# The gated one-hot columns of the expert gates spread over ScalarE, GpSimd and VectorE

## The chip, the cores and the metric

One NeuronCore of a Trainium2 chip runs the whole kernel in one launch. The metric is device microseconds of that core. The core's engines are TensorE (PE in the profile; its weight loads are PEld), VectorE (DVE), ScalarE (ACT), GpSimd (POOL) and SyncE (SP). Each works through its own queue in order and meets the others at semaphores.

## The reference, cut to what matters

A decoder trunk of two layers over 512 tokens of width 1024, in float32. Each layer has a token mixer (two kinds of attention) and then a PEER sub-layer: for every token, 8 heads each pick 16 of 128 x 128 = 16,384 experts, one expert being a row of `u` and a row of `v`.

```
expert_idx = i_top[..., 0] * 128 + i_top[..., 1]      # 8 heads x 16 picks = 128 picks a token
gates = softmax(best)
act = gelu(h . u[expert_idx]) * gates                 # one number a pick
out = sum over the picks of act * v[expert_idx]
```

Half of the tokens (256) are done by fetching the picked rows from DRAM. For the other half the kernel computes `gelu(u h)` for all 16,384 experts and multiplies it by a gate map: for a token, the gate map G[i, j] is the gate of expert (i, j), and zero where the expert was not picked. As each pick k has a first key i(k), a second key j(k) and a gate g(k), the map is a product of two matrices with the 128 picks as the contracted side: P[k, x] = (x == one key of pick k) * g(k), and Q[k, y] = (y == the other key of pick k). This change is about the making of P.

## The kernel before

**The stages of a layer.** After the token mixer, `channel_mix` runs on every engine. TensorE (1) turns 64 of the 128 tiles of `u` and multiplies them with the tokens (`act_tiles`), (2) makes the gate maps of the 256 dense tokens (`gate_maps`), (3) multiplies the gated activations with 64 tiles of `v` (`value_tiles`), (4) does the other 64 tiles of `u`, and (5) the other 64 of `v`. The change touches stage 2 alone.

**The gate stage.** 256 tokens are 32 batches (`NB`) of 8 (`BATCH`). For a batch, `p1` holds P (8 tokens x 128 columns, two buffers, `s = b % 2`) and `q1` holds Q in the same shape. `pqgT` holds, for each token, three columns with a value for each of the 128 picks on the partitions: the two keys and the gate; a fourth holds the negated gate. `iota` is a 128 x 128 tile with 0 to 127 along each row. Batch b runs like this:

- ScalarE, `p_batch` (lines 945 and 949): P of tokens 0 to 5 (`P_ACT = 6`), two operations a token: Abs(key - iota), a drain, then Relu(gate - gate * that), which is the gate where the keys agree and zero elsewhere.
- VectorE, `q_batch` (lines 1425, 1427, 1431): P of tokens 6 and 7 in two `tensor_tensor` operations over both tokens (equal, and times the gate), and Q of all 8 tokens in one `tensor_tensor` of 1024 columns.
- TensorE (line 588) waits for `p_done`, `q_done`, `gm_done` and `gs_done`, multiplies 8 pairs of matrices (16 instructions in the profile) into two PSUM banks and counts `g_done`.
- VectorE, `gate_batch` (line 1441): multiplies the 64 columns of the present half into the activations, straight out of PSUM. ScalarE, `keep_batch` (line 961), copies the other half to SBUF afterwards, and SyncE writes it to DRAM for stage 4.

P and Q of batch b wait until TensorE is done with batch b - 2, whose buffer they take. VectorE's order is P and Q of batch b, gate of batch b - 1, one row, and so on; ScalarE's is P of batch b, copy of batch b - 1.

**The fetched rows.** Between all this VectorE works off 512 rows a layer (1024 columns each): a row of `u` with a multiply-and-sum (line 1408), a row of `v` with a multiply-add (line 1414) and a drain. GpSimd fetches them by an indirect DMA each (line 1155) into a ring of 8: the fetch of row r waits until row r - 8 is used up. In the gate stage VectorE does one row a batch: row 164 + b in batch b. At row 192 (batch 28) it also has a `topk` of some thirty small operations to do.

**After the stage.** Rows 196 to 367 are done beside stages 3 and 4. From row 368 on (`kept_maps`, line 1458) VectorE multiplies the kept half of the gate maps into the second half of the activations, for which it waits until TensorE has made them.

Of the kernel before, what the change touches and what calls it, by code (L numbers as in the profile page):

```python
# [25 lines left out]
ALU = mybir.AluOpType  # L26
# [3 lines left out]
P = 128  # L30
# [25 lines left out]
ND = CH - GCH  # L56
# [3 lines left out]
STREAM = 4  # L60
STREAMED = 2 * TILES
BATCH = 8
P_ACT = 6
NB = NT // BATCH
BLOCKS = 4
G_START = 302
# [46 lines left out]
def build(nc, io, out):  # L113
    with ExitStack() as ctx:
        def sb(name, shape, dt=F32):
            return ctx.enter_context(nc.sbuf_tensor(name, shape, dt))

        def sem(name):
            return ctx.enter_context(nc.semaphore(name))
# [76 lines left out]
        p1 = mod[:, SHIFT1:GAIN1 + 1, :]  # L196
# [7 lines left out]
        pqgT = h_row[:, :].rearrange("p (a b) -> p a b", a=4)  # L204
        at = [A_TOPK]

        def small(*dims):
# [29 lines left out]
        iota = sb("iota", [P, P])  # L237
# [5 lines left out]
        S = {n: sem(n) for n in (  # L243
            "c_in const_in x_in c_sig_done c_act_done zeros_done layer_done small_in lam_summed lam_exped g_in "
            "norm_gain bias_in mod_mm mod_evac acc_done sq_done sq2_done norm_h tr_done hT_ev "
            "q_ev k_ev v_ev dqraw_ev dkraw_ev dv_mm dv_ev rope_mm dq_ready dk_ready "
            "z_done  ln_done L_done b_done w_exp w_masked pv_done ysb_ev "
            "s_done max_done p_exp dw_done wt_done wt_ev y_done y_sq yn_done yt_done yd_ev "
            "sig_done merged_done wout_in wo_done x_upd "
            "query0_done qst0_ev sc0_done sc0_ev query_done qst_ev sc_done sc_ev topk_done gate_exp dots_done gelu_done "  # L250
            "row_used st_used ut_done ut_ev a_used a_ev iota_mm iota_ev td_done exp_t_done pre_done pt_done pq_ev p_done q_done g_done gm_done gs_done kept_used "
            "x_out x_back out_sq out_ready out_done "
            "parked_act parked_dve parked_pool parked_pe parked_sp").split()}
        ada_in = [sem(f"ada_in{i}") for i in range(3)]
# [199 lines left out]
        def _(pe):  # L454
# [123 lines left out]
            def gate_maps(l):  # L578

                with pe.Fori(0, NB // 2) as g:  # L580
                    for s in range(2):
                        b = NB * l + 2 * g + s
                        pe.wait_ge(S["p_done"], b + 1)
                        pe.wait_ge(S["q_done"], b + 1)
                        pe.wait_ge(S["gm_done"], b + 1)
                        pe.wait_ge(S["gs_done"], b + 1)
                        for t in range(BATCH):
                            last = pe.matmul(ps[:, G_BANK[s] + t // 4, t % 4 * P:(t % 4 + 1) * P],  # L588
                                             p1[:, s, t * P:(t + 1) * P], q1[s][:, t * P:(t + 1) * P], start=True, stop=True)
                        last.then_inc(S["g_done"], 1)  # L590
# [174 lines left out]
            with pe.Fori(0, DEPTH) as l:  # L765
# [10 lines left out]
                with pe.Fori(0, MT // 2) as m2:  # L776
                    for s in range(2):
# [3 lines left out]
                        for b, (k0, n, rhs) in enumerate(((0, KD, hT), (KD, KD, hT), (16, 4, y_sb), (20, 4, y_d))):  # L781
                            for k in range(n):
                                last = pe.matmul(ps[:, 4 * s + b, :], w_m[:, s, k0 + k, :], rhs[:, k, :],  # L783
                                                 start=(k == 0), stop=(k == n - 1))
# [30 lines left out]
                act_tiles(l, 0, 8 * (HEADS - 2), HALF)  # L815
                turn_picks(l)
                gate_maps(l)
                value_tiles(l, 0)
                turn_u(l, 1, 0)
# [5 lines left out]
        def _(act):  # L825
            def park():
                act.sem_inc(S["parked_act"], 1)
# [110 lines left out]
            def p_batch(l, b):  # L938
# [3 lines left out]
                park()  # L942
                for t in range(P_ACT):
                    n = BATCH * b + t
                    act.activation(p1[:, s, t * P:(t + 1) * P], iota[:, :], ACT.Abs, bias=pqgT[:, 1, n:n + 1], scale=-1.0)  # L945
                act.drain()
                for t in range(P_ACT):
                    n = BATCH * b + t
# [173 lines left out]
        @block.gpsimd  # L1122
        def _(pool):
            def park():
                pool.sem_inc(S["parked_pool"], 1)

            with pool.Fori(0, DEPTH) as l:
                with pool.Fori(0, TURNS) as t:
                    i = l * TURNS + t
                    for u in range(2 * CH):  # L1130

                        pool.wait_ge(S["w_exp"], 8 * i + u + 1)
                        park()
                        pool.affine_select(out=w_att[:, u % 2, 0:P], in_=w_att[:, u % 2, 0:P], compare_op=ALU.is_gt,  # L1134
                                           fill=0.0, base=0, pattern=[[1, P]], channel_multiplier=-1
                                           ).then_inc(S["w_masked"], 1)
                def read_kept(r, half):
                    slot = r % KEPT
                    pool.wait_ge(S["kept_used"], 2 * NB * l + NB * half + r + 1)
                    park()  # L1140
                    if half == 0 and r < KEPT:
                        pool.wait_ge(kept_out[slot], 16 * (NB // KEPT) * l + 16 * (NB // KEPT))
                        park()
                    pool.dma_start(kept[slot], gate_dram[:, r, :].rearrange("p (a n) -> p a n", a=2)).then_inc(kept_in[slot], 16)

                def block(n, table, j):
                    for k in range(TOPK):
                        r = TOPK * n + k
                        if r in range(KEEP0, KEEP0 + NB):
                            read_kept(r - KEEP0, 0)  # L1150
                        if r in range(KEEP1, KEEP1 + NB):
                            read_kept(r - KEEP1, 1)
                        pool.wait_ge(S["row_used"], UNITS * ROWS * l + r + 1)
                        park()
                        pool.indirect_dma_start(out=ring[:, r % RING, :], out_offset=None, in_=table,  # L1155
                                                in_offset=bass.IndirectOffsetOnAxis(ap=idx[:, j % 4, k:k + 1], axis=0)
                                                ).then_inc(row_in[r % RING], 16)

                for j in range(UNITS):
                    pool.wait_ge(S["topk_done"], l * UNITS + j + 1)  # L1160
                    park()
                    block(max(2 * j - 1, 0), io["u"], j)
                    if j > 0:
                        block(2 * j, io["v"], j - 1)
                block(2 * UNITS - 1, io["v"], UNITS - 1)


        @block.vector
        def _(dve):
            def park():  # L1170
                dve.sem_inc(S["parked_dve"], 1)
# [243 lines left out]
                                                 ALU.mult, ALU.add).then_inc(S["row_used"], 1)  # L1415
                        dve.drain()

            def q_batch(l, b):

                s, n = b % 2, BATCH - P_ACT  # L1420
                of, rest = slice(BATCH * b, BATCH * (b + 1)), slice(BATCH * b + P_ACT, BATCH * (b + 1))
                dve.wait_ge(S["g_done"], NB * l + b + G_START - 1)
                park()
                p = p1[:, s, P_ACT * P:BATCH * P].rearrange("p (t i) -> p t i", t=n)
                dve.tensor_tensor(p, iota[:, :].unsqueeze(1).broadcast_to([P, n, P]),
                                  pqgT[:, 1, rest].unsqueeze(2).broadcast_to([P, n, P]), ALU.is_equal)
                dve.tensor_tensor(q1[s].rearrange("p (t i) -> p t i", t=BATCH),
                                  iota[:, :].unsqueeze(1).broadcast_to([P, BATCH, P]),
                                  pqgT[:, 0, of].unsqueeze(2).broadcast_to([P, BATCH, P]), ALU.is_equal)
                dve.drain()  # L1430
                dve.tensor_tensor(p, p, pqgT[:, 2, rest].unsqueeze(2).broadcast_to([P, n, P]),
                                  ALU.mult).then_inc(S["q_done"], 1)

            def gate_batch(l, b):

                bank = G_BANK[b % 2]
                dve.wait_ge(S["g_done"], NB * l + b + G_START + 1)
                park()
                acts = act_t[:, :, BATCH * b:BATCH * (b + 1)]
                gate = ps[:, bank:bank + 2, :].rearrange("p a (t i) -> p (a t) i", t=4)[:, :, 0:HALF]  # L1440
                dve.tensor_tensor(acts, acts, gate.rearrange("p t i -> p i t"), ALU.mult).then_inc(S["gm_done"], 1)

            def gate_maps(l, row0):

                for b in range(NB):
                    q_batch(l, b)
                    if b >= 1:
                        gate_batch(l, b - 1)
                    rows(l, row0 + b, row0 + b + 1)
                gate_batch(l, NB - 1)  # L1450
# [201 lines left out]
```

## Time and profile before

| | |
|---|---|
| runs (3) | 4058.1 us median, 4056.68 to 4061.71 |
| the profiled execution | 4059.52 us, its span 4057.8 us |
| PE busy | 3633.8 us, 90% of the span |
| DVE busy | 2603.7 us, 64% |
| ACT busy | 1116.9 us, 28% |
| POOL busy | 1433.5 us, 35% |
| granted TensorE clock, mean | 0.95 of full speed |

A view by line gives, for a group of like instructions, how often it ran, its busy time and the mean of one. A timeline line gives the start in microseconds from the begin of the span, the length, the engine, the line of the code, the operation, what it writes and reads, and in square brackets how long the engine was idle before it and what ended that. "x6" are six instructions drawn as one, so their length is from the first start to the last end. PE's ends are modelled, and POOL's spans are rough.

### The profile page before, as it was taken

The page shows a single profiled execution, that of the slowest core. Times are in us where ns is not written, and L with a number is a line of the kernel's source. Part 1 is how long each engine was busy: PE and PEld are TensorE (multiplying, and loading weights), DVE is VectorE, ACT ScalarE, POOL GpSimd, SP SyncE. Part 2 cuts the span into 40 slices and gives each one's busy share as a digit, 9 for nine tenths or more (in the row PEclk, how much of TensorE's full clock was granted, in tenths as well). Part 3 has the DMA queues.
Part 4 walks back from the last instruction along what each step waited for, and adds up shares of the span by engine and source line. Part 5 has one row for each costly group of instructions (what it writes and reads, how often), then busy time and mean ns, then how long its engine had stood idle before and what let it go on. Part 6 is the DMA issues. An engine that isn't in the chain of part 4 may idle for free.

```text
span 4057.8 us, 51253 instructions
## 1 busy us (share of the span) xinstructions
PE 3633.8 (90%) x13950; PEld 2299.6 (57%) x13950; DVE 2603.7 (64%) x5393; ACT 1116.9 (28%) x2531; POOL 1433.5 (35%) x1220
## 2 busy tenths in 40 slices
PE   4999898999866999998979998989998579999987
PEld 2444444777654448873445454457767544588633
DVE  6444214898987777676654451169998777676665
ACT  1333211323287003330023231023224940133100
POOL 0000001445433665566500000014544345656663
PEclk9999999999977999999989998999998789999999
DMA  6221122888855999999942212248877579999997
GB/s 246 102 104 47 66 100 104 306 317 310 301 161 174 405 399 395 341 373 384 389 187 93 93 43 98 79 173 319 315 296 270 162 256 401 405 380 346 384 386 308
DMA packets 278115, 1016.53 MB, mean 251 GB/s; under 512 B 31354, under 2 KB 48250, under 8 KB 266882
## 3 DMA queue, kind: packets, MB, share of 16 engines
q0 software_dynamic: 157696, 570.50, 37.5%
q1 hardware_dynamic: 120194, 443.42, 29.0%
q8 instruction: 94, 1.54, 0.2%
q14 instruction: 131, 1.07, 0.1%
HBM read 988.63 MB, written 25.17 MB: 250 GB/s over the span
## 4 chain that ended last, share of the span: by engine, by line
PE 48%; DVE 22%; DMA 10%; ACT 7%; issue 6%; DVEq 5%; POOL 1%; ACTq 1%; SPq 0%; POOLq 0%
PE ps L604 16%; PE ps L783 8%; PE ps L557 6%; DMA arena<-in_u_dram,idx 5%; DVE mod L1414 4%; PE ps L515 4%; DVE arena L1408 3%; DVE arena L1196 3%; ACT mod L949 2%; ACT mod L945 2%; PE ps L658 2%; DMA hT<-gate_scratch 2%; DMA arena<-in_v_dram,idx 2%; PE ps L492 2%; PE ps L612 2%
## 5 line engine op out<-in xcount | busy, mean ns | idle before, releaser
L1155 POOL DMA_INDIRECT arena<-in_u_dram,idx x512 | 665.5, 1300 | 986.4 <-issue 656.9
L557 PE MATMUL ps<-hT,mod 128*128 128x256 f32 x4096 | 926.9, 379 | 0.0
L604 PE MATMUL ps<-arena 128*128 128x512 f32 x2048 | 888.3, 597 | 33.4 <-DVE arena L1458 29.7
L1155 POOL DMA_INDIRECT arena<-in_v_dram,idx x512 | 650.4, 1270 | 633.9 <-DVE mod L1414 379.7
L557 PEld LDWEIGHTS ps<-hT,mod 128*128 128x128 f32 x4096 | 759.6, 190 | 93.0
L1408 DVE CUSTOM_DVE_ANT_0 arena<-arena 128x1024 f32<-128x1024 f32 x512 | 616.4, 1224 | 248.2 <-DMA arena<-in_u_dram,idx 244.8
L1414 DVE SCALAR_TENSOR_TENSOR mod<-arena,mod 128x1024 f32<-128x1024 f32 x512 | 657.1, 1283 | 139.0 <-DMA arena<-in_v_dram,idx 110.9
L604 PEld LDWEIGHTS ps<-arena 128*128 128x128 f32 x2048 | 391.7, 191 | 527.5 <-issue 527.4
L977 ACT COPY mod<-ps 128x512 f32<-128x512 f32 x512 | 274.6, 590 | 555.9 <-PE ps L547 555.5
L1134 POOL TENSOR_SCALAR_AFFINE_SELECT arena<-arena 128x128 f32<-128x128 f32 x64 | 19.9, 311 | 824.9 <-ACT arena L1055 824.9
L547 PE MATMUL ps<-const,arena 128*128 128x128 f32 x2048 | 269.0, 275 | 16.3 <-ACT mod L977 15.5
L547 PEld LDWEIGHTS ps<-const,arena 128*128 128x128 f32 x2048 | 239.0, 141 | 47.4 <-ACT mod L977 22.9
L524 PE MATMUL ps<-hT,arena 128*128 128x512 f32 x512 | 232.0, 613 | 14.8 <-DMA arena<-in_w_q_dram 12.5
L1196 DVE SCALAR_TENSOR_TENSOR arena<-arena,c_act 128x256 f32<-128x256 f32 x448 | 213.6, 484 | 41.1 <-DMA arena<-in_ada_w_dram 9.4
L783 PE MATMUL ps<-hT,arena 128*128 128x512 f32 x512 | 228.5, 605 | 2.7 <-ACT arena L1084 2.7
L1542 DVE TENSOR_TENSOR arena<-arena,ps 128x512 f32<-128x512 f32 x32 | 22.0, 688 | 307.0 <-PE ps L783 307.0
L515 PE MATMUL ps<-hT,arena 128*128 128x512 f32 x416 | 188.2, 607 | 3.2 <-ACT hT L859 1.9
L910 ACT ACTIVATE arena<-ps 128x512 f32<-128x512 f32 x128 | 76.9, 601 | 370.8 <-PE ps L557 370.8
L524 PEld LDWEIGHTS ps<-hT,arena 128*128 128x128 f32 x512 | 100.5, 197 | 137.2 <-issue 136.6
L783 PEld LDWEIGHTS ps<-hT,arena 128*128 128x128 f32 x512 | 99.3, 194 | 128.4 <-issue 128.4
L588 PE MATMUL ps<-arena,mod 128*128 128x128 f32 x512 | 93.8, 358 | 79.1 <-ACT mod L949 57.7
L588 PE MATMUL ps<-cos_sin,mod 128*128 128x128 f32 x512 | 94.4, 360 | 70.1 <-ACT mod L949 70.1
(196 smaller groups left out, 3715.4 us busy)
## 6 DMA issues: line engine op xcount, KB each, us to landing
arena<-in_u_dram SPq DMA_DIRECT2D x256, 512.0 KB
arena<-in_v_dram SPq DMA_DIRECT2D x256, 512.0 KB
arena<-in_ada_w_dram SPq DMA_DIRECT2D x56, 1024.0 KB, 6.0
hT<-gate_scratch POOLq DMA_DIRECT2D x128, 256.0 KB, 10.5
arena<-in_w_qkv_dram SPq DMA_DIRECT2D x48, 512.0 KB, 6.2
arena<-in_w_m_dram SPq DMA_DIRECT2D x16, 1536.0 KB, 6.7
arena<-in_w_q_dram SPq DMA_DIRECT2D x32, 576.0 KB, 6.7
gate_scratch<-hT SPq DMA_DIRECT2D x64, 256.0 KB, 2.1
```

Of the source, the lines that this page charges most:

```text
L515: last = pe.matmul(ps[:, bank, :], w_qkv[:, g, k, :], hT[:, k, :], start=(k == 0), stop=(k == KD - 1))
L524: last = pe.matmul(ps[:, c, :], q_w[:, c, k, :], hT[:, k, :], start=(k == 0), stop=(k == KD - 1))
L547: last = pe.transpose(ps[:, 4 + h, k * P:(k + 1) * P], stream[:, slot, kk * P:(kk + 1) * P], C(IDENT))
L557: last = pe.matmul(ps[:, 6 + tile // 2 % 2, tile % 2 * NT:(tile % 2 + 1) * NT], u_turned[:, tile % 2, k * P:(k + 1) * P], hT[:, k, DT0:SEQ ...
L588: last = pe.matmul(ps[:, G_BANK[s] + t // 4, t % 4 * P:(t % 4 + 1) * P], p1[:, s, t * P:(t + 1) * P], q1[s][:, t * P:(t + 1) * P], start=T ...
L604: last = pe.matmul(ps[:, 2 * c + n, :], act_t[:, e, c * P:(c + 1) * P], stream[:, slot, n * 512:(n + 1) * 512], start=(half == 0 and e == ...
L783: last = pe.matmul(ps[:, 4 * s + b, :], w_m[:, s, k0 + k, :], rhs[:, k, :], start=(k == 0), stop=(k == n - 1))
L977: act.copy(u_turned[:, tile % 2, h * 512:(h + 1) * 512], ps[:, 4 + h, :]).then_inc(S["ut_ev"], 1)
L1155: pool.indirect_dma_start(out=ring[:, r % RING, :], out_offset=None, in_=table, in_offset=bass.IndirectOffsetOnAxis(ap=idx[:, j % 4, k:k + ...
L1196: last = dve.scalar_tensor_tensor(acc, ada_w[at % 3][:, k, :], c_act[:, k:k + 1], bias[:, cols] if k == 0 else acc, ALU.mult, ALU.add)
L1408: dve.tensor_tensor_reduce(row, row, h2[:, j % 2, :], 1.0, 0.0, ALU.mult, ALU.add, dots[:, j % 2, k:k + 1]).then_inc(S["row_used"], 1)
L1414: dve.scalar_tensor_tensor(total, row, coef[:, k:k + 1], total, ALU.mult, ALU.add).then_inc(S["row_used"], 1)
```

## The change

ScalarE now makes P of tokens 0 to 2 (`P_ACT = 3`). GpSimd makes P of tokens 3 to 5 in a new `columns(b)`, and VectorE P of tokens 6 and 7 in its own `columns`, both with one `tensor_scalar` a token (equal to the key, then times the gate, both taken from a column with one value a partition). Q is made as before. TensorE waits for one more semaphore, `pp_done`. GpSimd's work for batch b stands in its queue ahead of the fetch of row 168 + b.

```diff
-P_ACT = 6
+P_ACT = 3
+P_DVE = 6
@@ gate_maps of TensorE
                         pe.wait_ge(S["p_done"], b + 1)
+                        pe.wait_ge(S["pp_done"], b + 1)
                         pe.wait_ge(S["q_done"], b + 1)
@@ GpSimd
+                def columns(b):
+                    s = b % 2
+                    if b == 0:
+                        pool.wait_ge(S["pq_ev"], ND * l + ND)
+                        park()
+                    pool.wait_ge(S["g_done"], NB * l + b + G_START - 1)
+                    park()
+                    for t in range(P_ACT, P_DVE):
+                        n = BATCH * b + t
+                        last = pool.tensor_scalar(p1[:, s, t * P:(t + 1) * P], iota[:, :], pqgT[:, 1, n:n + 1],
+                                                  pqgT[:, 2, n:n + 1], ALU.is_equal, ALU.mult)
+                    last.then_inc(S["pp_done"], 1)
...
                 def block(n, table, j):
                     for k in range(TOPK):
                         r = TOPK * n + k
+                        if r in range(168, 168 + NB):
+                            columns(r - 168)
@@ VectorE
-                p = p1[:, s, P_ACT * P:BATCH * P].rearrange("p (t i) -> p t i", t=n)
-                dve.tensor_tensor(p, iota[:, :].unsqueeze(1).broadcast_to([P, n, P]),
-                                  pqgT[:, 1, rest].unsqueeze(2).broadcast_to([P, n, P]), ALU.is_equal)
                 dve.tensor_tensor(q1[s].rearrange("p (t i) -> p t i", t=BATCH),
...
-                dve.drain()
-                dve.tensor_tensor(p, p, pqgT[:, 2, rest].unsqueeze(2).broadcast_to([P, n, P]),
-                                  ALU.mult).then_inc(S["q_done"], 1)
+                for t in range(P_DVE, BATCH):
+                    n = BATCH * b + t
+                    last = dve.tensor_scalar(p1[:, s, t * P:(t + 1) * P], iota[:, :], pqgT[:, 1, n:n + 1], pqgT[:, 2, n:n + 1],
+                                             ALU.is_equal, ALU.mult)
+                last.then_inc(S["q_done"], 1)
```

## Rows read from the trace of the kernel before

**Rows 1.** Busy time in a stretch, by engine; then granted clock, DMA share, GB/s.
```profile
1129.00:1300.00 171.00, 94.64 (x516) 86.84 (x515) 130.87 (x214) 154.51 (x426) 52.95 (x34) 0.73 0.51 158
3126.00:3297.00 171.00, 94.47 (x513) 86.75 (x514) 130.62 (x215) 154.46 (x426) 53.31 (x34) 0.73 0.51 157
```
**Rows 2.** Waits in 1130 to 1300: who for whom, us in total, times, longest.
```profile
PE ps L588 <- ACT mod L949: 63.8, 31, 5.5
```
**Rows 3.** Timeline, begin of the gate stage of the first layer.
```profile
1130.40 1.86 ACT L945 ACTIVATE mod<-iota,h_row 128x128 f32<-128x128 f32 x6 [0.21 <-issue]
...
1134.81 3.78 PE L588 MATMUL ps<-cos_sin,mod 128*128 128x128 f32 x16 [5.54 <-ACT mod L949]
```
**Rows 4.** Timeline, one batch of the stage, with a row of `v`.
```profile
1149.14 2.05 PE L588 MATMUL ps<-arena,mod 128*128 128x128 f32 x16 [1.24 <-ACT mod L949]
1149.46 1.86 ACT L945 ACTIVATE mod<-iota,h_row 128x128 f32<-128x128 f32 x6
1150.14 0.42 DVE L1425 TENSOR_TENSOR mod<-iota,h_row 128x256 f32<-128x256 f32 x1 [0.20 <-issue]
1150.48 1.22 DVE L1427 TENSOR_TENSOR cos_sin<-iota,h_row 128x1024 f32<-128x1024 f32 x1
1150.77 1.75 POOL L1155 DMA_INDIRECT arena<-in_v_dram,idx  x1 [3.51 <-DVE mod L1414]
1151.39 2.42 ACT L949 ACTIVATE mod<-mod,h_row 128x128 f32<-128x128 f32 x6
1151.77 0.42 DVE L1431 TENSOR_TENSOR mod<-mod,h_row 128x256 f32<-128x256 f32 x1
1152.12 0.68 DVE L1441 TENSOR_TENSOR arena<-arena,ps 128x512 f32<-128x512 f32 x1
1152.71 1.28 DVE L1414 SCALAR_TENSOR_TENSOR mod<-arena,mod 128x1024 f32<-128x1024 f32 x1
1153.72 0.56 ACT L961 COPY hT<-ps 128x512 f32<-128x512 f32 x1
1153.86 3.42 PE L588 MATMUL ps<-cos_sin,mod 128*128 128x128 f32 x16 [2.67 <-ACT mod L949]
1154.19 0.43 DVE L1425 TENSOR_TENSOR mod<-iota,h_row 128x256 f32<-128x256 f32 x1 [0.20 <-issue]
```
**Rows 5.** Timeline of VectorE, two batches following each other, with a row of `u`.
```profile
1197.47 0.42 DVE L1425 TENSOR_TENSOR mod<-iota,h_row 128x256 f32<-128x256 f32 x1
...
1201.18 0.42 DVE L1425 TENSOR_TENSOR mod<-iota,h_row 128x256 f32<-128x256 f32 x1
```
**Rows 6.** Timeline: begin and end of the topk of batch 28, and the stage's end.
```profile
1270.50 0.16 DVE L1389 RECIPROCAL arena<-arena 128x1 f32<-128x1 f32 x1
...
1280.27 1.28 DVE L1414 SCALAR_TENSOR_TENSOR mod<-arena,mod 128x1024 f32<-128x1024 f32 x1
...
1294.28 3.64 PE L588 MATMUL ps<-arena,mod 128*128 128x128 f32 x16 [2.06 <-ACT mod L949]
...
1299.78 2.54 PE L604 MATMUL ps<-arena 128*128 128x512 f32 x4 [1.86 <-ACT hT L961]
```
**Rows 7.** Timeline of ScalarE in batch 16: the first of two table loads, and what follows them.
```profile
1211.37 1.28 ACT L916 ACT_TABLE_LOAD   x1
...
1214.50 1.85 ACT L945 ACTIVATE mod<-iota,h_row 128x128 f32<-128x128 f32 x6
```
**Rows 8.** VectorE's groups by line and shape: a `tensor_scalar` with two scalars by column.
```profile
L1283 DVE TENSOR_SCALAR arena<-arena,rz,neg_lam 128x128 f32<-128x128 f32 x8 | 2.8, 346 | 0.6
```
**Rows 9.** VectorE's line 1233: ns min/median/max, first and last start.
```profile
L1233 DVE TENSOR_TENSOR arena<-arena,cos_sin x16: 691/758/825, 127.7 to 2414.3; 128x512 f32<-128x512 f32 x16
```
**Rows 10.** Timeline: a GpSimd operation (line 1134) and one of line 1233 together.
```profile
127.68 0.29 POOL L1134 TENSOR_SCALAR_AFFINE_SELECT arena<-arena 128x128 f32<-128x128 f32 x1 [2.69 <-ACT arena L1055]
127.68 0.82 DVE L1233 TENSOR_TENSOR arena<-arena,cos_sin 128x512 f32<-128x512 f32 x1 [0.16 <-issue]
```
**Rows 11.** Timeline, the begin of `kept_maps` in the first layer.
```profile
1662.60 0.60 DVE L1458 TENSOR_TENSOR arena<-arena,hT 128x256 f32<-128x256 f32 x1 [15.85 <-ACT arena L910]
```

More of the change, by code:

```diff
@@ L250, in build @@
             "query0_done qst0_ev sc0_done sc0_ev query_done qst_ev sc_done sc_ev topk_done gate_exp dots_done gelu_done "
-            "row_used st_used ut_done ut_ev a_used a_ev iota_mm iota_ev td_done exp_t_done pre_done pt_done pq_ev p_done q_done g_done gm_done gs_done kept_used "
+            "row_used st_used ut_done ut_ev a_used a_ev iota_mm iota_ev td_done exp_t_done pre_done pt_done pq_ev p_done pp_done q_done g_done gm_done gs_done kept_used "
             "x_out x_back out_sq out_ready out_done "
@@ L1416, in rows, with columns @@
                         dve.drain()
-            def q_batch(l, b):
-                s, n = b % 2, BATCH - P_ACT
-                of, rest = slice(BATCH * b, BATCH * (b + 1)), slice(BATCH * b + P_ACT, BATCH * (b + 1))
+            def columns(l, b):
+                s = b % 2
                 dve.wait_ge(S["g_done"], NB * l + b + G_START - 1)
                 park()
-                p = p1[:, s, P_ACT * P:BATCH * P].rearrange("p (t i) -> p t i", t=n)
-                dve.tensor_tensor(p, iota[:, :].unsqueeze(1).broadcast_to([P, n, P]),
-                                  pqgT[:, 1, rest].unsqueeze(2).broadcast_to([P, n, P]), ALU.is_equal)
                 dve.tensor_tensor(q1[s].rearrange("p (t i) -> p t i", t=BATCH),
                                   iota[:, :].unsqueeze(1).broadcast_to([P, BATCH, P]),
-                                  pqgT[:, 0, of].unsqueeze(2).broadcast_to([P, BATCH, P]), ALU.is_equal)
-                dve.drain()
-                dve.tensor_tensor(p, p, pqgT[:, 2, rest].unsqueeze(2).broadcast_to([P, n, P]),
-                                  ALU.mult).then_inc(S["q_done"], 1)
+                                  pqgT[:, 0, BATCH * b:BATCH * (b + 1)].unsqueeze(2).broadcast_to([P, BATCH, P]), ALU.is_equal)
+                for t in range(P_DVE, BATCH):
[3 more added lines that the diff above has]
+                last.then_inc(S["q_done"], 1)
             def gate_batch(l, b):
@@ L1445, in gate_maps @@
                 for b in range(NB):
-                    q_batch(l, b)
+                    columns(l, b)
                     if b >= 1:
```

## The prediction

> **What bounds the kernel now.** I read the busy time by stretch first, then who waits for whom, then the timeline of a few batches. The two gate stages last from 1130.4 and 3127.1 until the first `v` tile, some 169.4 us each (1299.78 - 1130.40 in the first [rows 3, 6]), and in them ScalarE is the busiest engine: 154.5 us of 171, against 130.9 of VectorE, 94.6 of TensorE and 53.0 of GpSimd [rows 1]. TensorE waits 63.8 us in 31 waits for ScalarE's line 949, the second operation of P [rows 2]: about once a batch.
>
> One batch shows why. TensorE starts every 4.72 us (1153.86 - 1149.14), and ScalarE's queue is full for that time: 1.93 us from the first Abs to the first Relu, 2.33 us on to the copy, and some 0.46 to the next Abs [rows 4]. VectorE could go round in less: with a row of `v` 4.05 us (1154.19 - 1150.14, without a stall in it) [rows 4], with a row of `u` 3.71 us (1201.18 - 1197.47) [rows 5]. TensorE's 16 instructions take 2.05 us at the higher clock and 3.42 to 3.78 us at the lower [rows 3, 4]; the mean granted clock of the stage is 0.73 [rows 1].
>
> The stage, as a sum that the new one can be held against: first batch 4.41 (1134.81 - 1130.40) [rows 3], 31 steps of 4.72 = 146.3, the tail from the last batch to the first `v` tile 5.50 (1299.78 - 1294.28) [rows 6], and a rest of 13.2, which is the topk of batch 28 and the two table loads of batch 16. Does time saved here last? At the next place where VectorE's rows meet TensorE's tiles, the begin of `kept_maps`, VectorE stands idle for 15.85 us until activations come that TensorE has still to make [rows 11]. Rows and tiles both follow the stage's end, so both move up by the same, and I count the saving in full.
>
> **ScalarE.** Half of six Abs and half of six Relu go. From the row lengths (1.86 us for six, 2.42 for six [rows 4]) three cost about 0.95 and 1.2, so P falls from 4.26 to about 2.25 us, and with the copy the round is 4.72 - 2.0 = 2.7 us. ScalarE is then no bound. The two table loads still hold it for 3.13 us (1214.50 - 1211.37) [rows 7], but with over a microsecond to spare in each batch I count 1.5 of it.
>
> **VectorE.** It becomes the bound. Lines 1425 and 1431 go: from start to start 0.34 (1150.48 - 1150.14) and 0.35 (1152.12 - 1151.77), with a drain in between. Of the 1.98 us from line 1425 to 1441, about 1.14 stay for Q, if it overlaps its follower by 0.08 as its neighbours do [rows 4]. Added are two `tensor_scalar` of 128 columns with two scalars by column, 346 ns each alone [rows 8] and about 0.27 from start to start by the same overlap: 0.54. So P and Q go from 1.98 to 1.68, and the round from 4.05 and 3.71 to 3.75 and 3.41; as 16 of the 32 rows are of `v` and 16 of `u`, the mean is 3.58. From both sides: 0 to 0.35 us for each of the two.
>
> **GpSimd.** Its three `tensor_scalar` a batch are the unknown; the trace has none. The nearest row is line 1134, one input, 128 columns: 0.29 us [rows 10]. These have two scalars by column more, and no reason makes them cheaper, so the lower end is 0.29; the upper end I take from the costliest thing that GpSimd does here, a fetch, 1.75 us when something stands in its way [rows 4]. I take 0.4 from start to start. A batch costs GpSimd then 1.2 + the fetch 1.75 + about 0.3 between them = 3.3 us, below VectorE's 3.6, and it can start on batch b the moment TensorE is done with b - 2, as in that stretch nothing before it in the queue still waits: the fetch ahead of it needs a row used several batches earlier. Behind it waits the fetch of row 168 + b, while VectorE is at row 164 + b: four batches ahead, some 16 us, where it was seven. I count nothing for that, nor for the DMA queues, which carry the same transfers (DMA share 0.51 in the stage [rows 1]).
>
> **What the two do to each other.** The fetch of 1.75 us began at 1150.77, under line 1427, which ended at 1151.70; it ended at 1152.52, 0.82 us after that [rows 4]. It reads its list of rows from SBUF, and waits while VectorE reads two SBUF inputs. The other way round: line 1233 takes 691 ns at best and 825 at worst, with the median 758 just between, so half of its 16 are long [rows 9]; a long one is the one that begins with GpSimd's 128-column operation [rows 10]. So a GpSimd operation of this size, 0.29 us long, costs VectorE 0.13 us, not its whole length. Three a batch that all hit are 0.40 us; some fall under line 1441, which has one input in PSUM, but the two `tensor_scalar` of VectorE may suffer more than a two-input one, and the scalars are read too. I add 0.4: 3.98 us a batch, with 0 and 3 x 0.4 = 1.2 as the ends. The Trainium skill, page "SBUF — State Buffer", section "Who interferes with whom", says that the pair of SBUF ports shared by VectorE and GpSimd is an exclusive lock held for the whole instruction, the other blocking fully. That speaks against this change. By that rule VectorE would lose three times the whole GpSimd operation; the rows show the lock, but the loss at less than half of the length.
>
> **TensorE.** At the lower clock its batch is up to 3.78 us [rows 3]. With a hand-over at each end (0.05 us from the last Relu's end, 1151.39 + 2.42, to 1153.86 [rows 4]; I take 0.2 for both) such a round cannot be under 4.0, as VectorE gets from the columns of one batch to its line 1441 only when that batch's matmuls are done. The clock is between its levels on the mean, so even a VectorE without any loss gives some 3.8 rather than 3.58. Together I take 4.05 us.
>
> **The sum.** First batch: ScalarE's 2.25 plus some 0.2, 2.5. 31 x 4.05 = 125.6. The topk takes VectorE 9.77 us (1280.27 - 1270.50) [rows 6] and, as VectorE is the bound now, all of it shows: 9.8. Table loads 1.5, tail 5.5. That is 144.9, against 169.4: 24.5 us a layer, 49 us in two, the second stage being alike to a fraction of a microsecond [rows 1]. The profiled execution took 4059.5 us; it would take 4010.5. That execution lies 1.4 above the median of the three runs, so 4009.
>
> **The rivals.**
> - *The whole of each GpSimd operation is lost to VectorE.* 3.58 + 3 x 0.4 = 4.8, less what line 1441 covers, about 0.4: 4.4 us a batch. Stage 155.7, saving 2 x 13.7 = 27: 4031. For it: the fetch did wait for all of VectorE's instruction. Against: the 0.13 us of rows 9 and 10. The page above gives this one.
> - *No loss at all, and TensorE mostly at the higher clock.* 3.65 us a batch, stage 132.5, saving 74: 3984. For it: GpSimd's work begins as line 1441 does; TensorE would be busier in the stage. Against: the long ones of line 1233.
> - *GpSimd becomes the bound (the other side).* Place: `pp_done`, which TensorE waits for. Its batch is 3 x s + 2.05 us with s the start-to-start time of one `tensor_scalar`. The stage is as long as before where 31 T + 19.3 = 169.4, T = 4.84, so s = 0.93. At s = 1.2, T is 5.65; the topk then shows with about 8 and the table loads not at all: 191, which is 22 us a layer more: 4102. For it: two scalars by column and a comparison are not what line 1134 does, and the fetch beside it is blocked by a VectorE that is busier than before. Against: 0.29 us for the same 128 columns, a third of what it takes. The Trainium skill, page "GPSIMD Engine Reference", section "Performance versus the Vector engine", puts a good one-input loop at about 1.8 cycles an element at 1.2 GHz; estimated from it 128 elements are 0.19 us before the fixed part. No run here shows that.
> - *It doesn't do what it says*, that is, ScalarE's part stays the bound for another reason, or GpSimd's late P gives back just what ScalarE's gave: 4.72 to 4.9 us a batch, 4050 to 4062.
>
> **How the numbers follow.** The forecast (3.85 to 4.25 us a batch, 3997 to 4022) 0.50, the first rival and what lies beside it 0.22, the second 0.10, the third 0.13, the last 0.05. Faster by over 0.2% (about 8 us, what a measurement of this kernel can tell from none) is the forecast and the first two rivals, less 0.01 for the first one's upper edge: 0.81. Within 0.2%: the last one and that edge, 0.06. Slower: the third, 0.13. The range leaves out the lower half of the second rival and the third: 3985 to 4056.
>
> **What would show it.** Right: line 949 gone from TensorE's waits in the stage, VectorE nearly without idle time in a batch, starts of line 588 about 4.05 us apart, first `v` tile at 1275. GpSimd's `tensor_scalar` 0.3 to 0.5 us; Q's operation (line 1427 before, 1.22 us) sometimes 0.1 to 0.3 longer. For the first rival: VectorE's operations longer by the whole of GpSimd's. For the third: TensorE waits for GpSimd, VectorE for TensorE in line 1441, and the fetches drift behind. Wrong in the rest: if the stretch after the stage grows by what the stage lost, the 15.85 us of slack at `kept_maps` was not what I took it for.

## The result and the profile after

The changed kernel took 4065.5 us (median of 20 runs, 4058.2 to 4073.8) against 4057.4 us (20 runs, 4052.4 to 4063.5) of the kernel before on the same chips. The ratio is 1.0020, 95% interval 1.0013 to 1.0027: slower by some 5 to 11 us, where 49 us less had been forecast. The profiled execution took 4065.7 us, its span 4064.0 us.

In a second comparison on another chip (after_again, below) the ratio was 1.0015, with an interval across 1.

First the busy times of the page, then the two gate stages by engine (the counterpart of [rows 1]; PE, PEld, DVE, ACT, POOL, then granted clock, DMA share, GB/s).

```profile
PE 3635.4 (89%) x13950; PEld 2304.2 (57%) x13950; DVE 2597.8 (64%) x5393; ACT 992.5 (24%) x2147; POOL 1653.4 (41%) x1412
```

```profile
1129.00:1300.00 171.00, 94.44 (x511) 88.33 (x510) 126.82 (x213) 91.31 (x232) 151.29 (x127) 0.75 0.47 142
3129.00:3300.00 171.00, 94.63 (x512) 88.52 (x510) 126.81 (x212) 91.16 (x232) 151.09 (x127) 0.75 0.47 141
```

ScalarE fell from 154.5 to 91.3 us as reckoned, and GpSimd rose from 53.0 to 151.3: it has taken ScalarE's place as the engine that is busy nearly all the time. The waits of the stage (the counterpart of [rows 2]) say the same. TensorE hardly waits for ScalarE's second operation any more; GpSimd's line 1157, its new `tensor_scalar`, stands there, and VectorE in turn waits for TensorE in the gate multiply (line 1456), ScalarE for VectorE in the copy (line 963).

```profile
ACT hT L963 <- DVE arena L1456: 74.4, 30, 10.9
...
PE ps L590 <- POOL mod L1157: 50.8, 14, 6.4
DVE arena L1456 <- PE ps L590: 37.8, 14, 4.3
```

The begin of the first stage, the counterpart of [rows 3]. ScalarE has its three tokens done at 1134.75 + 1.26 = 1136.0, but GpSimd takes until 1133.75 + 5.07 = 1138.8, so the first batch starts 5.22 us after the first Abs and not 2.5 as forecast, or 4.41 as before.

```profile
1133.69 0.99 ACT L947 ACTIVATE mod<-iota,h_row 128x128 f32<-128x128 f32 x3 [0.22 <-issue]
1133.75 5.07 POOL L1157 TENSOR_SCALAR mod<-iota,h_row 128x128 f32<-128x128 f32 x3 [21.68 <-ACT h_row L936]
1134.75 1.26 ACT L951 ACTIVATE mod<-mod,h_row 128x128 f32<-128x128 f32 x3
...
1138.91 3.75 PE L590 MATMUL ps<-cos_sin,mod 128*128 128x128 f32 x16 [6.36 <-POOL mod L1157]
```

Two GpSimd turns in the middle of the stage: the first while VectorE stands idle, the second beside a row of `u` (line 1425), Q (1440) and VectorE's own two `tensor_scalar` (1445).

```profile
1207.25 2.36 POOL L1157 TENSOR_SCALAR mod<-iota,h_row 128x128 f32<-128x128 f32 x3
```

```profile
1209.71 2.02 PE L590 MATMUL ps<-arena,mod 128*128 128x128 f32 x16
1209.78 1.03 POOL L1172 DMA_INDIRECT arena<-in_u_dram,idx  x1 [0.17 <-issue]
...
1210.51 1.22 DVE L1425 CUSTOM_DVE_ANT_0 arena<-arena 128x1024 f32<-128x1024 f32 x1
...
1210.85 6.05 POOL L1157 TENSOR_SCALAR mod<-iota,h_row 128x128 f32<-128x128 f32 x3
...
1211.65 1.22 DVE L1440 TENSOR_TENSOR cos_sin<-iota,h_row 128x1024 f32<-128x1024 f32 x1
...
1212.79 0.76 DVE L1445 TENSOR_SCALAR mod<-iota,h_row 128x128 f32<-128x128 f32 x2
...
1217.00 2.26 PE L590 MATMUL ps<-cos_sin,mod 128*128 128x128 f32 x9 [5.26 <-POOL mod L1157]
```

Undisturbed, three operations take 2.36 us: 0.79 each, about twice the 0.4 I had taken and nearly three times the 0.29 of [rows 10]. Beside a busy VectorE they take 6.05, and TensorE starts 0.1 us after they end, 7.29 us after its last start. Over both stages the average of the 192 is 1.19 us an operation. With a fetch (1.22 and 1.25 us on the mean for rows of `u` and `v` in the stage) and 0.2 between, that is 3 x 1.19 + 1.45 = 5.0 us a batch. Measured: the 31 steps of the first stage are 161.5 us, the one with the topk 13.4, so the other 30 are 4.94 on average. The same mean of the kernel before is 4.89 ((159.5 - 12.8) / 30); its 4.72 is the usual step, without the table loads' one.

Against the sum before: first batch 5.22 (4.41), 31 steps 161.5 (159.5), tail 3.88 (5.50), together 170.6 us (169.4). The tail is shorter as the last batch fell on the higher clock. In a second profile (below) the stages are 175.6 and 171.2. The mean of the four is 172.0, 2.6 more than before, 5.2 in two layers. That is the lower edge of what the runs show, and no run places the other part: in the first profile the stage also begins 3.3 us later, after code that is the same, but this place scatters from 1129.7 to 1134.5 over the kernels profiled here.

### The profile page after: what moved, and what is told of

Same layout as the page of the kernel before. It is cut to its first block, busy times and chain, and to the rows that moved or that the text cites. A ratio compares the mean times of both kernels' runs of the same rounds, so it can differ in the third digit from the quotient of the medians.

```text
span 4064.0 us, 51133 instructions
## 1 busy us (share of the span) xinstructions
PE 3635.4 (89%) x13950; PEld 2304.2 (57%) x13950; DVE 2597.8 (64%) x5393; ACT 992.5 (24%) x2147; POOL 1653.4 (41%) x1412
## 4 chain that ended last, share of the span: by engine, by line
PE 49%; DVE 22%; DMA 9%; issue 7%; POOL 6%; DVEq 5%; ACT 1%; POOLq 0%; ACTq 0%; SPq 0%
PE ps L606 16%; PE ps L785 8%; PE ps L558 6%; DMA arena<-in_u_dram,idx 4%; PE ps L516 4%; DVE arena L1425 4%; POOL mod L1157 3%; DVE mod L1431 3%; DVE arena L1213 3%; PE ps L660 2%; DMA arena<-in_v_dram,idx 2%; POOL arena L1172 2%; DMA hT<-gate_scratch 2%; PE ps L493 2%; PE ps L614 2%
## 5 line engine op out<-in xcount | busy, mean ns | idle before, releaser
L1157 POOL TENSOR_SCALAR mod<-iota,h_row 128x128 f32<-128x128 f32 x192 | 226.7, 1186 | 61.9 <-ACT h_row L936 42.2
```

Source lines behind the costliest of these rows:

```text
L1157: last = pool.tensor_scalar(p1[:, s, t * P:(t + 1) * P], iota[:, :], pqgT[:, 1, n:n + 1], pqgT[:, 2, n:n + 1], ALU.is_equal, ALU.mult)
```

## Experiments

All are variants of the changed kernel. "6/0/2" is how many of the eight tokens ScalarE, GpSimd and VectorE have. As the kernel before took between 4057 and 4092 us on different chips, each ratio is against its runs on the same chip; the stage is from the profile, from the first Abs to the first `v` tile in each layer, and the median step is that of the first layer. imm and width32 are one execution each, without a ratio.

| label | split | stages, us | median step, us | ratio to before, 95% |
|---|---|---|---|---|
| (before) | 6/0/2, old form | 169.4, 169.5 | 4.72 | |
| (after) | 3/3/2 | 170.6, 170.6 | 4.60 | 1.0020 (1.0013 to 1.0027) |
| after_again | 3/3/2 | 175.6, 171.2 | 4.86 | 1.0015 (0.9987 to 1.0042) |
| act6_vec2 | 6/0/2 | 166.8, 168.8 | 4.73 | 0.9988 (0.9964 to 1.0012) |
| act3_vec5 | 3/0/5 | 152.6, 152.7 | 4.50 | 0.9925 (0.9897 to 0.9952) |
| act5_vec3 | 5/0/3 | 152.5, 152.1 | 4.05 | 0.9924 (0.9897 to 0.9950) |
| act4_vec4 | 4/0/4 | 148.6, 148.4 | 4.25 | 0.9901 (0.9864 to 0.9937) |
| act4_vec4_again | 4/0/4 | 148.6, 148.6 | 4.25 | 0.9882 (0.9847 to 0.9917) |
| act5_pool1_vec2 | 5/1/2 | 151.5, 154.3 | 4.05 | 0.9931 (0.9906 to 0.9956) |
| act4_pool1_vec3 | 4/1/3 | 142.1, 142.1 | 3.99 | 0.9824 (0.9790 to 0.9858) |
| act4_pool2_vec2 | 4/2/2 | 135.1, 135.5 | 3.73 | 0.9808 (0.9771 to 0.9845) |
| drain_u | 3/3/2 and drains | 163.9, 163.1 | 4.86 | 0.9951 (0.9923 to 0.9979) |
| imm | 3/3/2, constants | 150.6, 151.2 | 4.18 | |
| width32 | 3/3/2, 32 columns | 140.4, 139.9 | 3.74 | |

**Is it GpSimd?** Its share goes to VectorE, or only VectorE's new form stays.

```diff
-P_DVE = 6
+P_DVE = 3        # act3_vec5; act6_vec2 has P_ACT = 6 instead, P_DVE stays 6
@@ TensorE, gate_maps
-                        pe.wait_ge(S["pp_done"], b + 1)
@@ GpSimd, block
-                        if r in range(168, 168 + NB):
-                            columns(r - 168)
```

act3_vec5:

> ScalarE three tokens, VectorE five, GpSimd none. Theory (GpSimd's late columns set the pace of the gate stage): VectorE bounds at 1.14 + 5 x 0.26 + 0.60 + 1.34 = 4.4 us a batch, TensorE's waits for GpSimd are gone, 31 x 4.4 + 19.3 = 155.7 us a stage against 169.4, so 4058 - 27 = 4030 us. Rival (TensorE's lower clock and the hand-overs between three engines hold the stage, whoever makes the columns): as the changed kernel, 4065 us, line 590 still some 4.9 us apart.

act6_vec2:

> VectorE's part of the change alone: one tensor_scalar a token for two tokens, ScalarE six tokens as before, GpSimd none. Theory (ScalarE was the bound before, GpSimd is after): no change, 4.72 us a batch, within 3 us of the kernel before. Rival (the new form on VectorE costs more than the two tensor_tensor and is what makes the changed kernel slow): slower than before by 4 us or more.

Measured: 152.7 us a stage with five tokens on VectorE (expected 155.7; before 169.4), the first batch 2.54 us after the first Abs, so the same 3 tokens of ScalarE are fine once GpSimd is out of it, and neither TensorE nor the hand-overs hold the stage. VectorE's form alone makes no difference that can be told (0.9988, interval across 1). The loss is GpSimd's part.

**What of GpSimd's 0.79 us is what?** One execution each, with another operation in place of that of line 1157 (cut to one line each). imm compares with constants and width32 writes 32 of the 128 columns, so neither makes the P of the reference, and only their times count:

```diff
-pool.tensor_scalar(p1[:, s, t * P:(t + 1) * P], iota[:, :], pqgT[:, 1, n:n + 1], pqgT[:, 2, n:n + 1], ALU.is_equal, ALU.mult)
+pool.tensor_scalar(p1[:, s, t * P:(t + 1) * P], iota[:, :], 1.0, 2.0, ALU.is_equal, ALU.mult)              # imm
+pool.tensor_scalar(p1[:, s, t * P:t * P + 32], iota[:, 0:32], pqgT[:, 1, n:n + 1], pqgT[:, 2, n:n + 1], ALU.is_equal, ALU.mult)   # width32
```

imm:

> GpSimd's three operations take the two constants 1 and 2 instead of two scalars by column, so its P columns are not the reference's; all else as in the changed kernel. Theory (the two scalars by column make the difference between 0.79 us and the 0.29 us of line 1134): 0.3 to 0.45 us each where nothing blocks it. Rival (comparison and multiply on 128 columns cost it that much themselves): 0.7 to 0.8 us.

width32:

> GpSimd's three operations are 32 columns wide instead of 128, so a part of P is not written; all else as in the changed kernel. Theory (a fixed cost for the scalars and the start): 0.65 us or more of the 0.79 stay. Rival (a cost by column, 0.79 / 128 = 6 ns each): 0.2 to 0.35 us.

The line's minimum, median and maximum in ns, with the first and last start, in the changed kernel, in imm and in width32:

```profile
L1157 POOL TENSOR_SCALAR mod<-iota,h_row x192: 780/804/2787, 1133.7 to 3299.0; 128x128 f32<-128x128 f32 x192
```

```profile
L1157 POOL TENSOR_SCALAR mod<-iota x192: 632/670/1725, 1133.2 to 3261.9; 128x128 f32<-128x128 f32 x192
```

```profile
L1157 POOL TENSOR_SCALAR mod<-iota,h_row x192: 463/484/2666, 1133.3 to 3253.5; 128x32 f32<-128x32 f32 x192
```

Each came out between its theory and its rival. The two scalars by column cost 0.15 us (780 - 632), where the theory needed 0.35 to 0.5; 96 columns cost 0.32 us (780 - 463), 3.3 ns each. If the cost is a straight line through these two widths, 128 columns are 0.42 of the 0.78 and 0.36 is fixed. Line 1134, one input and also 128 columns, is 0.29 in all: another operation on the same engine and shape was no measure for this one. The stages show how steep it is: 0.32 us less an operation made the stage 30 us shorter. With GpSimd at 0.48 it is 140.2 us, below the 144.9 that I had reckoned with 0.4.

**Does it matter where they wait?**

```diff
                         if k == TOPK - 1:
                             dve.drain().then_inc(S["dots_done"], 1)
+                        elif 164 <= n < 196:
+                            dve.drain()
```

drain_u:

> The changed kernel with a drain of VectorE behind each row of u in the gate stage, as there already is behind each row of v. Theory (GpSimd's read gets in only where VectorE's two-input operations leave a gap; behind a row of u there was none, and its operation stood through the row, Q and sometimes the two tensor_scalar, 2.5 to 2.8 us): none of GpSimd's operations over 2 us any more, the pairs of batches 14 to 27 fall from some 10.9 to 9.6 us, 4065 - 2 x 7 x 1.3 = 4047 us or so. Rival (GpSimd's own 0.79 us and the sum of its work bound the stage, where they wait makes no difference; the drain only lengthens VectorE's round by 0.2): 4065 us or up to 6 more.

```profile
L1157 POOL TENSOR_SCALAR mod<-iota,h_row x192: 780/804/1867, 1132.0 to 3298.0; 128x128 f32<-128x128 f32 x192
```

The longest is 1.87 us instead of 2.79, 24 operations over 2 us became none, and the 12 steps from batch 14 to 26, all beside rows of `u`, went from 62.4 to 58.0 us on the mean of the two layers, 9.7 a pair as expected, while VectorE does more than before. A part of the wait moved over to VectorE: its Q is 1.34 us on the mean, 1.26 without the drains. The stage is 163.5 us, and the ratio 0.9951 against 1.0015 and 1.0020 without the drains. So GpSimd's wait is not only for the operation that is under way: beside a row of `u`, Q begins 0.08 us before the row ends (1211.65 against 1210.51 + 1.22), and GpSimd's first operation came to its end only at 1213.5, 0.6 us after Q's; after a row of `v` there is a gap of 0.2 us, and it got in there. The trace of the changed kernel says the same without a drain: all 24 operations over 2 us (2.45 to 2.79) lie across a row of `u` and Q, while the 20 that lie across a row of `v` and Q took 1.87 at most, and those that met no Q all took 0.78 to 0.81.

**A smaller share.** Only `P_ACT`, `P_DVE` and where GpSimd has none the lines shown above differ.

act5_vec3:

> ScalarE five tokens, VectorE three, GpSimd none. Theory: ScalarE 4.72 - 0.71 = 4.01 us a batch, VectorE 1.14 + 3 x 0.26 + 1.94 = 3.9, TensorE at its lower clock 4.0: 4.05 to 4.1, stage 145 to 147, 45 us less than before: 4013 us. Rival (TensorE and hand-overs hold the stage at 4.7 to 4.9): 4050 to 4065 us.

act4_vec4:

> ScalarE four tokens, VectorE four, GpSimd none. Theory (without GpSimd the larger of the two engines' rounds and TensorE's 4.0 set the pace): ScalarE 3.3, VectorE 1.14 + 4 x 0.26 + 1.94 = 4.12 us a batch; stage 147, 4013 to 4018 us, within 4 us of the split five to three. Rival: 4050 or more, if TensorE and hand-overs hold the stage.

act5_pool1_vec2:

> ScalarE five tokens, GpSimd one, VectorE two. Theory (GpSimd's share was too big, not the idea wrong): its batch is one operation of 0.8 to 2.6 us and a fetch of 1 to 1.75, under 4 us, so ScalarE's 4.01 bounds: 4012 to 4025 us. Rival (each wait for GpSimd is late, however small its share, as VectorE's two-input operations block it): 4035 us or more.

After these, four kernels on one chip. after_again:

> The changed kernel once more, beside the splits of this call on one chip. Theory (GpSimd bounds the gate stage): 4.9 us a batch on the mean, stage 170 to 171 us as in its first profile, 1.000 to 1.004 of the kernel before. Rival (its first profile was a disturbed one): a stage under 168 us.

act4_pool1_vec3:

> ScalarE four tokens, GpSimd one, VectorE three. Theory (one operation of GpSimd a batch is early enough, and TensorE's lower clock is the next bound): VectorE 1.14 + 3 x 0.26 + 1.94 + 0.1 = 4.0, ScalarE 3.3, TensorE 4.0: stage 145 to 148, at or 3 us below the split four to four, 0.989 to 0.991 of the kernel before. Rival (GpSimd's operation is late in each batch whatever its share): stage 152 or more, as with five, one and two.

act4_pool2_vec2:

> ScalarE four tokens, GpSimd two, VectorE two. Theory (GpSimd's batch is its operations at 1.2 us each with the waits, and a fetch of 1.25 with 0.2 around it): 2 x 1.2 + 1.45 = 3.9, just about TensorE's 4.0, with the long waits behind rows of u some 4.5 there: stage 150 to 158. Rival (it is the third engine's hand-over, not the load): about the same as with one token, 145 to 152, or as with three, 170.

act4_vec4_again:

> ScalarE four tokens, VectorE four, once more beside the others on one chip: stage 148 to 149 us, 0.988 to 0.992 of the kernel before, and 0.987 to 0.991 of the changed one.

With ScalarE at five tokens the step is 4.05 us, ScalarE's own round, with or without GpSimd. The stages of 5/0/3 came out 5 to 7 us above the 145 to 147 expected, and 5/1/2, at 0.9931, lies between its theory (up to 4025 us of 4058) and its rival (4035 or more). The trace of 5/0/3 shows where it went. Five of the first stage's steps, some beside rows of `u` and some beside rows of `v`, were 4.98 to 5.05 us, and each followed a batch that TensorE did at the lower clock, granted 0.50. One of the five:

```profile
1154.50 3.78 PE L589 MATMUL ps<-cos_sin,mod 128*128 128x128 f32 x16 [1.35 <-ACT mod L950]
...
1158.43 0.69 DVE L1453 TENSOR_TENSOR arena<-arena,ps 128x512 f32<-128x512 f32 x1 [0.88 <-PE ps L589]
...
1159.31 0.59 ACT L962 COPY hT<-ps 128x512 f32<-128x512 f32 x1 [0.82 <-DVE arena L1453]
...
1163.52 2.05 PE L589 MATMUL ps<-cos_sin,mod 128*128 128x128 f32 x16 [2.93 <-ACT mod L950]
```

VectorE's gate multiply waits for the slow batch, ScalarE's copy for the multiply, and ScalarE's next P is late by that much. The step with the two table loads is 7.3 us, 3.2 over the usual, where the prediction's sum had 1.5.

With four, two and two no engine is behind: 3.73 us a step, 135.3 us a stage, 34 less than before. That is the lowest ratio of all, 0.9808, and better than both kernels (0.9824 with four, one and three, also better than its expected 0.989 to 0.991, is not to be told from it). I had expected a stage of 150 to 158 us, since I put GpSimd at 3.9 and at 4.5 beside rows of `u`, and TensorE at 4.0. All were too high: only 5 of its 128 GpSimd operations were over 2 us, the steps beside rows of `u` were mostly 3.4 to 3.6 us, and the stage and a batch of it show the rest:

```profile
1138.00:1266.00 128.00, 71.37 (x499) 66.15 (x499) 116.18 (x207) 107.03 (x283) 108.70 (x95) 0.90 0.65 189
```

```profile
1161.36 2.05 PE L590 MATMUL ps<-cos_sin,mod 128*128 128x128 f32 x16 [1.76 <-ACT mod L951]
...
1162.26 2.50 POOL L1157 TENSOR_SCALAR mod<-iota,h_row 128x128 f32<-128x128 f32 x2
...
1164.92 1.03 POOL L1172 DMA_INDIRECT arena<-in_v_dram,idx  x1 [0.17 <-issue]
1165.02 1.28 DVE L1431 SCALAR_TENSOR_TENSOR mod<-arena,mod 128x1024 f32<-128x1024 f32 x1
1165.09 2.05 PE L590 MATMUL ps<-arena,mod 128*128 128x128 f32 x16 [1.68 <-ACT mod L951]
```

GpSimd's round is 2.50 + 1.03 + gaps = 3.7 here, the same as VectorE's. And TensorE's mean granted clock is 0.90, where it was 0.75 in the changed kernel: its batches take 2.30 us on average, against 2.95.

Does the saving last? From the first `v` tile to the last of the layer the kernel before took 737.0 and 736.0 us, the changed one 738.7 and 735.6, act4_vec4 741.1 and 735.3. The profiles of the three shortest stages have more: act4_pool2_vec2 761.8 and 758.9, act4_pool1_vec3 754.6 and 758.1, width32 756.4 and 748.7. But act6_vec2, whose stage was hardly shorter, has as much (763.7 and 759.6). The difference arises in all of them between the first 64 `v` tiles and the next, where tiles of `u` are fetched. The profiled executions of act4_pool2_vec2 (4039.4 us) and act4_pool1_vec3 (4050.0) were the slowest of their six (medians 4012.3 and 4013.5), which speaks for scatter and against something given back; no run isolates it.

## Why the prediction was wrong

- **What bounds the kernel now**: held. ScalarE, at 4.72 us a batch. act3_vec5 and act4_vec4 are 17 and 21 us a stage faster for tokens moved from it to VectorE.
- **ScalarE**: held. 0.98 + 1.26 us for P (0.95 and 1.2 reckoned).
- **VectorE**: its prices held, "It becomes the bound" did not: it stood waiting for TensorE for 37.8 us of the stage. Q stayed 1.22 us (median 1.224), the two `tensor_scalar` 0.60 together and 342 ns the median (346 in [rows 8]), and the round of act3_vec5, 4.50 us, is near the 4.4 put from it.
- **GpSimd**: this is the step that failed. "I take 0.4 from start to start": it is 0.79 alone and 1.19 on the mean of the stage. And "costs GpSimd then 1.2 + the fetch 1.75 + about 0.3": the three took 3.56 and the fetch 1.25. I had let the fetch be blocked, as the row showed it, but not the new operations, which read the same memory: beside VectorE they wait as the fetch did, 0.4 us each on average and up to 2.0.
- **What the two do to each other**: the right lock, priced on the wrong side. I counted what VectorE loses: little, 0.05 us on the mean of Q (1.26, 1.22 before) and 0.06 on that of its `tensor_scalar` (0.40, 0.34 the median), though single ones are longer by 0.34 (Q) and 0.6 (`tensor_scalar`). That is some 0.17 us a batch, where I had added 0.4. What GpSimd loses is larger and I put it at nothing. The rule that I weighed (Trainium skill, "SBUF — State Buffer", "Who interferes with whom") is that the loser blocks fully, whichever of the two it is. I had read it as a loss of VectorE only. The trace agrees with it on the side of GpSimd: up to 2.79 us for an operation of 0.79 (the row of line 1157 above). On VectorE's side the loss was less than the whole of GpSimd's operation, 0.6 us at most.
- **TensorE**: "such a round cannot be under 4.0" was wrong, even at the lower clock. In the changed kernel itself a batch of 3.75 us, granted 0.50, is followed by the next, without a wait, 3.59 us after its start. The hand-overs did not add up to a round there: VectorE makes the columns of the next batch before it multiplies the gate of this one. And in the shorter rounds of act4_pool2_vec2 the clock was granted more, 0.90.

```profile
1138.91 3.75 PE L590 MATMUL ps<-cos_sin,mod 128*128 128x128 f32 x16 [6.36 <-POOL mod L1157]
1142.50 3.04 PE L590 MATMUL ps<-arena,mod 128*128 128x128 f32 x16
```

- **The sum**: with the measured step in place of 4.05, the rest was near: the topk 8.5 (13.4 - 4.94) rather than 9.8, the tail 3.9 rather than 5.5. The first batch, 5.2 rather than 2.5, is the same mistake.
- **The rivals**: the third happened, "GpSimd becomes the bound", place and mechanism as described, at 0.13; its size did not. 4065 is far from its 4102 and just beyond the 4050 to 4062 of the last rival, GpSimd giving back what ScalarE gave, at 0.05. I had its break-even at 0.93 us an operation, and it came at 1.19, for which its formula gives 5.6 us a batch and some 40 us of loss. The batch is 4.94, as the fetch that follows the operations seldom meets Q any more: 4 of the first stage's 35 began under it, where 31 of 33 had. It takes 1.22 to 1.25 us on the mean and not 1.75 (1.6 on the mean before). So the loss was 8 us.
- **Whether a saving lasts**: not tested by the change itself, as there was none. The faster splits bear it out as far as the scatter allows.

The range (3985 to 4056) left out all of the third rival. The price of an operation that no row shows, from 0.29 to 1.75 us, was in the text; the range did not follow from it.

## What to carry to other kernels

An operation moved to GpSimd needs its own duration: another of the same shape differed by almost three. And its blocked duration must be counted as well, in both directions, by how much of the round VectorE reads two SBUF inputs, and whether it ever leaves a gap. Before giving work to a third engine, set all rounds side by side with that number: here three tokens on GpSimd (3/3/2) were a loss of 0.2%, two (4/2/2) a gain of 1.9%, and none (4/0/4) a gain of 1.0 to 1.2%.

## What the runs showed of the hardware that I had not expected

- GpSimd's `tensor_scalar` (equal, multiply, float32, 128 columns): 0.78 us with two scalars by column, 0.63 with constants, 0.46 with 32 columns.
- It did not get between two VectorE instructions that overlap at their ends: 2.45 to 2.79 us beside a row of `u` and Q; a drain between them brought the longest to 1.87 us and the stage down by 7 to 8 us, though it costs VectorE 0.2 us each time.
- A fetch waits for Q in the same way: in the two gate stages of the kernel before, 63 of 67 began under line 1427's operation, and each ended 0.81 to 0.82 us after that operation's end.
- The same 16 instructions a batch were granted more clock where the rounds were shorter. With the mean of the first stage's steps without the topk's: 0.75 at 4.94 us (3/3/2), 0.77 at 4.40 (5/0/3), 0.83 at 4.05 (4/1/3), 0.84 at 3.96 (width32), 0.90 at 3.83 (4/2/2). The kernel before, 0.73 at 4.89, is the one a little out of line.
